# Nine opening matmuls for eighteen, the constants' fetch moved, and the sum over channels behind the values' last piece

## The reference, cut to what matters

```
xn = x * rsqrt(mean(x * x, channels) + EPS) * norm_mix_g
q, k, v, b_gate, c_gate, h, g_attn, g_conv = split(xn @ w_in)
q, k = rope(rmsnorm_per_head(q)), rope(rmsnorm_per_head(k))
# attention with a window of 128 and a sink per head; u = c_gate * h, a convolution of 3 taps
# gates and projections, x + merged @ w_out, then a SwiGLU layer on the norm of that
```

## Time and profile before

| | |
|---|---|
| three runs | 1733.05, 1734.26, 1735.46 us; median 1734.26 |
| profiled execution | 1733.39 us, its span 1731.60 us |
| TensorE matmul busy | 1714.1 us, 99% of the span |
| VectorE, ScalarE, POOL busy | 59%, 47%, 2% |
| HBM read | 299.5 MB, 175 GB/s over the span |
| granted TensorE clock, mean | 0.997 |

### The profile page before, as it was taken

How to read it: one execution, slowest core, us unless ns; L and a number is a source line. 1 busy time by engine, 2 the same in 40 slices (tenths; PEclk the granted TensorE clock), 3 DMA queues, 4 the chain that set the end, 5 groups by cost and what they waited for, 6 DMA issues and landing times.

```text
span 1731.6 us, 35651 instructions
## 1 busy us (share of the span) xinstructions
PE 1714.1 (99%) x13944; PEld 1699.0 (98%) x13944; DVE 1014.1 (59%) x1268; ACT 809.4 (47%) x985; POOL 31.5 (2%) x54
## 2 busy tenths in 40 slices
PE   8899999999999999999999999999999999999999
PEld 7899999999999999999999999999999999999999
DVE  7876776767754444555565655554455554455565
ACT  6445655455554444434444555543344443334443
POOL 0100000000000000000000000000000000000000
PEclk9899999999999999999999999999999999999999
DMA  7455455555566566556566555565556556556555
GB/s 241 152 159 158 145 157 158 162 153 158 157 213 185 178 181 179 176 175 186 160 194 193 164 177 182 170 192 175 179 171 186 176 175 187 175 177 183 174 176 153
DMA packets 298626, 302.73 MB, mean 175 GB/s; under 512 B 9488, under 2 KB 296336, under 8 KB 298464
## 3 DMA queue, kind: packets, MB, share of 16 engines
q1 hardware_dynamic: 296544, 296.00, 56.4%
q0 software_dynamic: 752, 3.80, 0.6%
q10 hardware_dynamic: 1296, 2.46, 0.5%
HBM read 299.50 MB, written 2.72 MB: 175 GB/s over the span
## 4 chain that ended last, share of the span: by engine, by line
PE 97%; DVE 1%; DMA 1%; issue 0%; ACT 0%; SPq 0%; DVEq 0%; ACTq 0%
PE acc L1007 31%; PE acc L1009 31%; PE acc L1008 31%; DMA raw<-in_w_in 1%; PE side L1104 1%; PE side L1128 0%; PE side L1116 0%; PE side L1092 0%; DVE w_lo L595 0%; DMA region_x<-in_x_t 0%; PE side L1106 0%; DVE region_m L661 0%; PE side L1118 0%; PE side L1131 0%; ACT w_hi L373 0%
## 5 line engine op out<-in xcount | busy, mean ns | idle before, releaser
L595 DVE TENSOR_TENSOR w_lo<-raw,w_hi 128x1024 fp32r<-128x1024 f32 x567 | 688.6, 1225 | 537.0 <-ACT w_hi L373 528.8
L373 ACT ACTIVATE w_hi<-raw 128x1024 fp32r<-128x1024 f32 x567 | 593.2, 1054 | 612.9 <-PE acc L1009 608.4
L1007 PE MATMUL acc<-xn_hi,w_hi 128*128 128x288 f32 x2976 | 855.2, 287 | 1.1 <-DVE w_lo L595 1.1
L1008 PE MATMUL acc<-xn_lo,w_hi 128*128 128x288 f32 x2976 | 851.9, 286 | 0.0
L1009 PE MATMUL acc<-xn_hi,w_lo 128*128 128x288 f32 x2976 | 851.9, 286 | 0.0
L1007 PEld LDWEIGHTS acc<-xn_hi,w_hi 128*128 128x128 f32 x2976 | 563.3, 189 | 2.5 <-issue 1.5
L1008 PEld LDWEIGHTS acc<-xn_lo,w_hi 128*128 128x128 f32 x2976 | 563.3, 189 | 0.1
L1009 PEld LDWEIGHTS acc<-xn_hi,w_lo 128*128 128x128 f32 x2976 | 563.2, 189 | 0.0
L1007 PE MATMUL acc<-at_hi,w_hi 128*128 128x288 f32 x1216 | 347.9, 286 | 0.5 <-DVE w_lo L595 0.5
L1008 PE MATMUL acc<-at_lo,w_hi 128*128 128x288 f32 x1216 | 347.8, 286 | 0.0
L1009 PE MATMUL acc<-at_hi,w_lo 128*128 128x288 f32 x1216 | 347.8, 286 | 0.0
(11 more groups left out here) (180 smaller groups left out, 755.1 us busy)
## 6 DMA issues: line engine op xcount, KB each, us to landing
raw<-in_w_in SPq DMA_DIRECT2D x199, 512.0 KB, 4.4
raw<-in_w_ffn_gate SPq DMA_DIRECT2D x88, 512.0 KB, 4.5
raw<-in_w_ffn_up SPq DMA_DIRECT2D x88, 512.0 KB, 4.4
raw<-in_w_ffn_down SPq DMA_DIRECT2D x64, 512.0 KB, 3.7
raw<-in_w_attn_proj SPq DMA_DIRECT2D x32, 512.0 KB, 4.5
raw<-in_w_conv_proj SPq DMA_DIRECT2D x32, 512.0 KB, 4.4
raw<-in_w_out SPq DMA_DIRECT2D x32, 512.0 KB, 4.6
raw<-in_w_ffn_down SPq DMA_DIRECT2D x32, 384.0 KB, 3.7
```

What stands on the lines that cost most here:

```text
L373: nc.scalar.activation(w_hi[:, s], raw[:, s], ACT.Copy).then_inc(S["hi_ready"], 1)
L595: V.tensor_tensor(w_lo[:, s], raw[:, s], w_hi[:, s].bitcast(F32), ALU.subtract).then_inc(S["lo_ready"], 1)
L1007: te.matmul(out, w_hi[:, s, k, cols], hi_b, start=first, stop=False)
L1008: te.matmul(out, w_hi[:, s, k, cols], lo_b, start=False, stop=False)
```

## The change

Three lines are edited. The number of matmuls on zeros goes from 18 to 9. POOL waits for the first load of `raw`'s last slot (the keys' weights, slot 3) before it fetches the constants, in place of slot 1's part of x. The matmul by ones stands behind the values' fourth piece, in place of the second.

```
-            pool.wait_ge(x_loaded[1], 16)
+            pool.wait_ge(raw_loaded[SLOTS - 1], 16)
             pool.dma_start(consts[:], constants).then_inc(S["consts_loaded"], 16)
...
-                for n in range(18):
+                for n in range(9):
                     te.matmul(acc[:, 2, :], weights[:, 0:P], moving[:, 0:512], start=True, stop=True)
...
             for s in range(SLOTS):
                 piece(G_V, s, 2, xn_hi, xn_lo)
-                if s == 1:
+                if s == SLOTS - 1:
                     pe.wait_ge(S["consts_loaded"], 16)
                     pe.wait_ge(S["x_sum_ready"], 1)
                     te.matmul(side[:, 2, 0:T], ones, x_square_sum, start=True, stop=True
                               ).then_inc(S["in_mean_in_psum"], 1)
```

## The result

| | kernel before | changed kernel |
|---|---|---|
| median, lowest, highest of 15 runs (us) | 1733.83, 1732.44, 1735.46 | 1737.59, 1736.77, 1738.94 |
| profiled execution, its span (us) | 1733.39, 1731.60 | 1738.69, 1736.9 |
| its mean granted TensorE clock | 0.997 | 0.994 |

The changed kernel is slower by 3.8 us: ratio 1.0024, 95% interval 1.0016 to 1.0032.

The account below looks back on a forecast made before the run. The prediction took the dependent line from L1062 to v_sample_t to bound the kernel: 3.3 (later L1062) + 1.0 (head sums) - 0.3 (given back) = +4.0 us, 1738.2 us against the median, range 1736.0 to 1740.6.

Parts of the forecast that it names:

- The line that ends in v_sample_t: Dependent steps from L1062 through the keys' square and head sums to v_sample_t before L1072; its delay moves the end.
- The rival in which TensorE's order sets the end: The wait before L1072 doesn't come through L1062; removed wait and earlier weights both gained: -3.3 us, 1731.0; chance 0.07.
- Opening matmuls at 0: Nine fewer matmuls on zeros at the start gain 0 us, since ScalarE's w_hi and the loads set the pace.
- the rival's upper end: Clock falls in the pause before the first group's second slot; L1062 +1.9 us more, at most 1740.2; chance 0.10.
- Constants worth 1.46 us: Later constants' fetch lets x's last part arrive sooner; ScalarE and VectorE work moves up by 1.46 us.
- L1062 at 34.0: Sum over channels, behind the values' fourth piece, runs at 34.0 in place of 30.69: 3.3 us later.
- The new wait of 5.7 us: TensorE waits 5.7 us before the head sums for the square of the keys, where two pieces stood.
- The head sums +1.0: After the new wait the head sums L1049 run at clock 0.50, 1.0 us later on the line.
- The rival in which the clock holds: Full clock through the wait before the head sums, which cost nothing extra: +3.0 us, 1737.3; chance 0.10.
- v_sample_t at 55.6: VectorE's v_sample_t, needed by L1072, comes 4.3 us later, at 55.6 in place of 51.30.
- What is given back, -0.3: Behind L1072 VectorE's w_lo sets the pace; a clock returning sooner gains at most 0.3 us, taken as -0.3.
- the loss side: If the clock comes back later behind the wait before L1072, up to a piece at half clock is lost.

Follow-up runs that it names:

- the three kernels in which the line starts earlier or is shorter: Kernel before with constants' fetch moved: 1732.23 us; plus VectorE's last three square additions before the third w_lo: 1731.75; plus ScalarE's query w_hi before the keys' root: 1730.77.
- the run with the new wait filled: Changed kernel with 24 matmuls on zeros between the sum over channels and the head sums: 1736.65 us, ratio 1.0020 to the kernel before.
- the runs with zeros in that wait: Matmuls on zeros ahead of the value rows: 24 in the kernel before, 1734.61 us; 20 in the kernel that gained 2.8 us, 1731.08 us.

## Why the prediction was right, point by point

**The line that ends in v_sample_t bounds the opening: right.** The sum moved alone costs 5.9 us, the constants and the opening matmuls don't cost anything, and the three kernels in which the line starts earlier or is shorter gain 1.6, 1.8 and 2.8 us (the first with an interval that just reaches no change). The rival in which TensorE's order sets the end would have given -3.3.

**Opening matmuls at 0: right.** With 18, 9 and 1 the changed kernel takes the same within what the runs can tell. The lost clock did occur in the profiled execution (0.50 from 12.74 to 16.15, behind a wait of 1.9 us), but its price was half a microsecond at L1062, not the 1.9 of the rival's upper end. There the values ran without any wait for w_lo, from 22.31 to 34.07. In the run with the new wait filled and in the one with nine opening matmuls alone, behind waits as long (1.94 and 1.91 us), the clock didn't fall.

**Constants worth 1.46 us: right.** The last part of x arrived at 14.71 (forecast 15.01) and the last slot's w_hi started at 16.43 (forecast 16.75) in an execution whose slot 1 arrived 0.29 early; counted from that arrival the w_hi came 1.49 earlier (7.59 us behind it in place of 9.08). Alone the edit moves L1062 by 1.6. The fetch landed at 22.3 (16.49 + 5.8), where about 24 was forecast; the sum needed it at 34.

**L1062 at 34.0: right, 34.07,** but so close by luck: two things that were not in the sum nearly cancel. The arrival was 0.29 early, and the clock in the opening cost 0.5. **The new wait of 5.7 us: right, 5.72. The head sums +1.0: right;** they took 1.2 more (2.29 against 1.09), the way from L1062 to L1072 1.0 more. The reason given was thinner than the result: the clock had lasted 2.16 us into the other wait, but it lasted 5.34 into this one, and with 0.38 us more the head sums would have begun at full clock. The rival in which the clock holds was that near in this execution; in the three other profiles with this wait unfilled and the sum behind the fourth piece the head sums took 2.29 too. **v_sample_t at 55.6: right, 55.65.**

**What is given back, -0.3: wrong in sign and in what sets the pace, and small.** I read from one execution that TensorE came to the fourth query piece 0.3 us behind its w_lo. In the changed kernel's profile that w_lo is done at 62.98 (the first of four that start at 61.75), and TensorE came at 64.12, 1.1 behind, since the clock stayed at 0.50 until 63.94. The prediction had named this as the loss side, but took VectorE to set the pace. In both profiles TensorE did: behind L1072 it ran at 0.50 for 8.01 us in place of 6.37, 1.64 us more, which at half pace is a loss of 0.82, and the stretch was 0.80 longer. VectorE's w_lo is the limit just below, which the runs with zeros in that wait reach (7.11 and 7.10 us). So between executions it is a matter of when the clock returns. From the first L1072 to the fourth query piece the kernels of the table that have no zeros there took 7.39 to 8.34 us; the kernel before's profile has the 7.39, the changed kernel's 8.19. That is 0.8 of the 5.3 us by which the two spans differ, where the medians stand 3.8 apart: both profiled executions lie off their medians, by -0.4 and by +1.1. The sum by steps that don't depend on it is 3.3 + 1.0 = 4.3, and L1072 moved by 4.36. That the whole forecast of +4.0 came within 0.2 us of the medians' 3.8 is thus partly luck; the line that it was built on is what the runs show.

## What to carry to other kernels

Work that stands between the start of a line of dependent steps and the place where its result is wanted is cover; a wait of 1.8 us there can be cheaper than none, because the two pieces behind it hid 5.7 us of other engines' time. Before a step is moved back to take away a wait, look for who waits for its result, in order, up to the next long wait of the busy engine: if that wait ends with the same line, the delay comes out at the end; here L1072 moved by 4.36 us and the medians by 3.8. And the gain lies the other way, in starting the line earlier and taking other work out of it.

## What the runs showed of the hardware

From the start of the fourth query piece to the end of the span every profiled execution but one took 1672.5 to 1672.9 us, whatever had happened before; the one exception lost the clock there. A pause of 1.9 us on TensorE was followed by a fall of the granted clock in one execution of the nine-matmul opening and not in two others, and in longer waits the clock held for 2.16 us in one execution and 5.34 in another, so one trace doesn't tell what a pause costs. One of the two others is the run with the new wait filled: the pause, and the clock from there to the sum over channels.

```profile
11.60 1.22 PE L1028 MATMUL acc<-xn_hi,w_hi 128*128 128x288 f32 x8 [1.94 <-ACT w_hi L373]
...
11.60:33.00 21.40, 20.81 (x165) 20.44 (x166) 16.62 (x20) 13.44 (x18) 1.44 (x2) 1.00 0.88 292
```

The fetch of the constants, issued by POOL amid VectorE's work both times, landed 7.4 us after its issue before and 5.8 us after it in the changed kernel:

```profile
consts<-in_constants POOLq DMA_DIRECT2D x1, 673.0 KB, 5.8
```

That agrees with the rule of the Trainium skill ("SBUF — State Buffer", "Who interferes with whom") by which tensor-tensor steps don't lock such a fetch out. It is no test of the rule: no run here had copies on VectorE at that time, and part of VectorE's work there was scalar-tensor-tensor steps (L610).
